# Output products between key pieces, weights requested first and a store awaited later in a decode step with windowed attention

## The reference

```python
# layer 0: latent attention | dilated window attention, one output projection
y = jnp.concatenate([o_mla, o_swa], axis=-1) @ w_out
# layer 1: gated short convolution
y = (b_gate * conv) @ w_out
# each layer
x = layer_norm(a*x + mixer(x)); x = layer_norm(a*x + mem_attend(x)); x = layer_norm(a*x + peer(x))

def dilated_group_attend(q_pos, q, kv_all, row0_pos, win, dil, bias):   # win, dil: (128,1) (512,4) (2048,16)
    s = jnp.einsum('bqhd,bqjhd->bhqj', q, kv[:, :, :, 0]) * SWA_SCALE + bias   # masked
    e = jnp.exp(s - m); den = e.sum(-1)
    o = jnp.einsum('bhqj,bqjhd->bqhd', e / den, kv[:, :, :, 1]); lse = m + log(den)

def mem_attend(x, kv, wq, wo):                       # 256 memory rows, 4 heads of 256
    s = jnp.einsum('bshd,bmhd->bhsm', x @ wq, kv[:, :, 0]) * MEM_SCALE
    return jnp.einsum('bhsm,bmhd->bshd', softmax(s), kv[:, :, 1]).reshape(B, S, D_MODEL) @ wo
```

## Time and profile before

| what | value |
|---|---|
| median of 3 runs | 2777.76 us (2771.65 to 2778.41) |
| the profiled execution, its own time | 2773.06 us |
| its span, first to last instruction | 2771.3 us |
| its mean granted TensorE clock | 0.972 |
| PE busy | 2592.0 us (94%) |
| DVE, ACT, POOL busy | 1428.2, 341.7, 621.0 us |
| moved by DMA | 885.35 MB, mean 319 GB/s |

### The profile page before, as it was taken

How to read it: one execution, slowest core, us unless ns; L and a number is a source line. 1 busy time by engine, 2 the same in 40 slices (tenths; PEclk the granted TensorE clock), 3 DMA queues, 4 the chain that set the end, 5 groups by cost and what they waited for, 6 DMA issues and landing times. The chain is left out here.

```text
span 2771.3 us, 40409 instructions
## 1 busy us (share of the span) xinstructions
PE 2592.0 (94%) x16081; PEld 2156.5 (78%) x16081; DVE 1428.2 (52%) x3384; ACT 341.7 (12%) x997; POOL 621.0 (22%) x619
## 2 busy tenths in 40 slices
PE   7889987799899999999999999988999999999997
PEld 5564464346399999999999866464999999999997
DVE  2430020122269979995555221222799799855553
ACT  3210120012021111110000010120211121100000
POOL 0005000000004324444333000000044244533330
PEclk9799998899999999999999999999999999999999
DMA  7789958996927999999999795769089899899995
GB/s 239 252 278 283 369 198 346 387 371 242 400 104 294 374 338 328 354 340 401 409 409 409 282 378 219 278 245 361 1 346 376 315 344 354 327 410 409 409 409 192
DMA packets 249128, 885.35 MB, mean 319 GB/s; under 512 B 27386, under 2 KB 34714, under 8 KB 238143
## 3 DMA queue, kind: packets, MB, share of 16 engines
q1 hardware_dynamic: 169374, 606.97, 58.7%
q0 software_dynamic: 79568, 275.81, 26.4%
HBM read 863.33 MB, written 109.08 MB: 351 GB/s over the span
## 5 line engine op out<-in xcount | busy, mean ns | idle before, releaser
L2891 PE MATMUL ps<-xT,front 128*128 128x192 f32 x4096 | 686.8, 327 | 3.5 <-DMA front<-in_peer_uT 2.9
L2891 PEld LDWEIGHTS ps<-xT,front 128*128 128x128 f32 x4096 | 663.1, 190 | 8.9 <-DMA front<-in_peer_uT 6.2
L2917 PE MATMUL ps<-p1e_S,p_qT 128*128 128x192 f32 x2048 | 336.9, 327 | 5.9 <-DMA p_qT<-in_peer_v 5.9
L2917 PE MATMUL ps<-p0e_S,p_qT 128*128 128x192 f32 x2048 | 337.0, 327 | 5.1 <-DMA p_qT<-in_peer_v 5.1
L2917 PEld LDWEIGHTS ps<-p1e_S,p_qT 128*128 128x128 f32 x2048 | 332.5, 190 | 10.0 <-DMA p_qT<-in_peer_v 10.0
L2917 PEld LDWEIGHTS ps<-p0e_S,p_qT 128*128 128x128 f32 x2048 | 332.4, 190 | 9.5 <-DMA p_qT<-in_peer_v 9.4
L2667 DVE CUSTOM_DVE_ANT_0 front<-front,x_tok 128x1024 f32<-128x1024 f32 x256 | 309.6, 1217 | 8.4 <-DMA front<-in_peer_u,p1e_expert 2.2
L2568 POOL DMA_INDIRECT front<-in_peer_u,p1e_expert x128 | 154.3, 1206 | 384.5 <-DVE p1e_dots L2667 200.7
L2568 POOL DMA_INDIRECT front<-in_peer_u,p0e_expert x128 | 154.0, 1203 | 385.0 <-DVE p0e_dots L2667 200.2
L2678 DVE SCALAR_TENSOR_TENSOR h_tok<-front,p1e_dots,h_tok 128x1024 f32<-128x1024 f32 x127 | 163.1, 1284 | 143.1 <-DMA front<-in_peer_v,p1e_expert 114.4
L2678 DVE SCALAR_TENSOR_TENSOR h_tok<-front,p0e_dots,h_tok 128x1024 f32<-128x1024 f32 x127 | 163.2, 1285 | 141.9 <-DMA front<-in_peer_v,p0e_expert 141.1
(11 more groups left out here) (474 smaller groups left out, 2855.1 us busy)
## 6 DMA issues: line engine op xcount, KB each, us to landing
front<-in_peer_uT SPq DMA_DIRECT2D x256, 512.0 KB
p_qT<-in_peer_v SPq DMA_DIRECT2D x256, 512.0 KB
out_swa_sample<-in_cache_swa_w SPq DMA_DIRECT2D x32, 2040.0 KB, 21.2
e_ring<-in_mla_pages SPq DMA_DIRECT2D x84, 272.0 KB, 4.6
e_ring<-in_swa_kT SPq DMA_DIRECT2D x16, 1024.0 KB, 7.8
e_arena<-in_swa_v SPq DMA_DIRECT2D x16, 1024.0 KB, 13.2
out_swa_sample<-in_cache_swa_w SPq DMA_DIRECT2D x8, 2016.0 KB, 31.1
e_ring<-in_attn_w_in SPq DMA_DIRECT2D x6, 2048.0 KB, 34.5
```

The source lines that it names most:

```text
L2891: mm = pe.matmul(k.ps[:, SB[i % len(SB)], 0:TD], ur[:, i % NU, c, :], k.xT[:, c, D0:T], start=(c == 0), stop=(c == KC - 1))
L2917: mm = pe.matmul(k.ps[:, c // 2, c % 2 * TD:(c % 2 + 1) * TD], vr[:, i % NV, c * P:(c + 1) * P], S[:, i, :], start=False, stop=(i == STEPS ...
```

## The change

Four edits in the layer 0 attention, and one in layer 1:

- The 16 products of a half are one sequence, cut over the twelve key pieces of the group: 11 of them behind pieces 2 to 12, one each (`products_beside`), and the last 5 behind the scores (`products_left`).
- The second half of the output weights is requested at the start of the sample stage, ahead of its first key request (`first`).
- The prompt stage no longer waits for its stores (`Stores` with due 0); the wait stands in the sample stage ahead of the first value request (`before_values`).
- The counts that the products wait for are given by hand: (64, 32).
- In layer 1 the ring "nx1" is allocated on the other side of the memory, and the room of the experts is opened before stage "nx1". Four key and two value transfers of the memory attention are requested there, behind load 2 (`load_early`); the prompt stage requests the other two values.

```diff
@@ joined_stage
                 ring.load(sp, n, job, i).then_inc(w_landed[n % NR], 16)
+                if beside_loads and n == beside_loads[0]:
+                    beside_loads[1](sp)
                 if n < len(copies):
                     k.copy_some(sp, copies[n])
@@ EarlyProjection
-    def product(self, pe, s, i):
-        pe.wait_ge(self.landed[s], self.due[s])
-        for c in range(KC):
-            mm = pe.matmul(self.k.ps[:, self.BANKS[i], :], self.aT[:, c, i * P:(i + 1) * P], self.pieces[s, c],
+    def products(self, pe, s, first, last):
+        for n in range(first, last):
+            i, c = divmod(n, KC)
+            if n == 0:
+                pe.wait_ge(self.landed[s], self.due[s])
+            mm = pe.matmul(self.k.ps[:, self.banks[i], :], self.aT[:, c, i * P:(i + 1) * P], self.pieces[s, c],
                            start=c == 0, stop=c == KC - 1)
-        mm.then_inc(self.tile_done, 1)
+            if c == KC - 1:
+                mm.then_inc(self.tile_done, 1)
+
+    def products_beside(self, pe, s, part, parts):
+        self.products(pe, s, part * self.BESIDE_SCORES // parts, (part + 1) * self.BESIDE_SCORES // parts)
+
+    def products_left(self, pe, s):
+        self.products(pe, s, self.BESIDE_SCORES, 2 * KC)
@@ attend_packed, SP
+            if a.get("first"):
+                a["first"](sp)
             for g in range(GROUPS):
                 for u in range(g * GB, (g + 1) * GB):
                     load_keys(u)
+                if g == 0 and a.get("before_values"):
+                    a["before_values"](sp)
                 for u in range(g * GB, (g + 1) * GB):
                     load_values(u)
-                if early and g == 0:
-                    early.load(sp, 1)
@@ attend_packed, PE
                     mm.then_inc(k_used, 1)
+                    if early:
+                        early.products_beside(pe, g, b * NPART + j, GB * NPART)
...
-                    if early and u == g * GB + 1:
-                        early.product(pe, g, 0)
                 if early:
-                    early.product(pe, g, 1)
+                    early.products_left(pe, g)
                     early.wait_taken(pe, g, 0)
@@ Stores
-        sp.wait_ge(self.sem, self.due)
+        if self.due:
+            sp.wait_ge(self.sem, self.due)
@@ even_mixer
-                    lambda sp: store_windows(k, kv, sp), k.window_stored, 16 * N_WINDOW_STORES,
+                    lambda sp: store_windows(k, kv, sp), k.window_stored, 0,
@@ swa_sample
-        "ahead": ahead, "early": early,
+        "ahead": ahead, "early": early, "first": lambda sp: early.load(sp, 1),
+        "before_values": lambda sp: sp.wait_ge(k.window_stored, 16 * N_WINDOW_STORES),
@@ MemoryCaches (new; load_keys and load_values as in memory_attention before)
+    def load_early(self, sp):
+        for u in range(self.keys_early):
+            self.load_keys(sp, u, u).then_inc(self.k.mem_keys_landed[u], 16)
+        for u in range(self.values_early):
+            self.load_values(sp, u, u).then_inc(self.k.mem_values_landed[u], 16)
@@ decode_step
-                ring = Ring(k, c2, "nx1", 3)
+                ring = Ring(k, c2, "nx1", 3, k.sb(rooms, "nx1_w", [P, 3, KC * 512], side="right"))
...
+                rooms.close()
+                room = ExpertRoom(k, rooms, 1)
+                caches = MemoryCaches(k, 1, room, keys_early=4, values_early=2)
                 joined_stage(k, "nx1", ring, conv_out, norm_of["mix"][1],
                              mid=[memory.values], last=[memory.queries], turn_at=1,
-                             copies=(0, 0, 2, 2, 2, 2))
+                             copies=(0, 0, 2, 2, 2, 2), beside_loads=(2, caches.load_early))
```

More of the change, by code:

```diff
@@ L374, in begin_next, with joined_stage @@
         self.ahead, self.first_slot = self.next_ahead, self.next_slot
-def joined_stage(k, name, ring, out_job, norm, mid=(), last=(), turn_at=0, memT=None, copies=(), zeros_behind=None, head=None, beside=None, next_job=None, rest=None):
+def joined_stage(k, name, ring, out_job, norm, mid=(), last=(), turn_at=0, memT=None, copies=(), zeros_behind=None, head=None, beside=None, next_job=None, rest=None, beside_loads=None):
     nc = k.nc
@@ L628, with __init__ @@
 class EarlyProjection:
-    BANKS = (4, 6)
-    def __init__(self, k, job, regions, first_due):
-        self.k, self.regions = k, regions
+    BESIDE_SCORES = 11
+    def __init__(self, k, job, banks, landed, due, regions):
+        self.k, self.regions, self.banks, self.landed, self.due = k, regions, banks, landed, due
         _, self.aT, self.w, self.chunk, _ = job
-        self.pieces, self.due = {}, [first_due, 0]
-        self.landed = [k.first_landed, None]
+        self.pieces = {}
         for s, region, c0, n in regions:
-            self.due[s] += 16
             for i in range(n):
@@ L2229, in load, with __init__, load_keys, load_values @@
         sp.dma_start(self.wq[n], src).then_inc(self.k.wq_landed[n], 16)
-def memory_attention(k, memory, ring, experts):
+class MemoryCaches:
+    def __init__(self, k, layer, room, keys_early=0, values_early=0):
+        self.k, self.layer, self.keys, self.values = k, layer, room.memory_keys, room.memory_values
+        self.keys_early, self.values_early = keys_early, values_early
+    def load_keys(self, sp, u, slot):
+        return sp.dma_start(self.keys[:, slot, :, :], self.k.io["mem_kT"][self.layer, u])
+    def load_values(self, sp, u, slot):
+        src = self.k.io["cache_mem_kv"][self.layer, u, :, 1].rearrange("(i p) h d -> p i (h d)", p=P)
+        return sp.dma_start(self.values[:, slot, :, :], src)
+    def load_early(self, sp):
[3 more added lines that the diff above has]
+            self.load_values(sp, u, u).then_inc(self.k.mem_values_landed[u], 16)
+    def load_ahead(self, sp):
+        for u in range(self.keys_early, 4):
+            self.load_keys(sp, u, u).then_inc(self.k.mem_keys_landed[u], 16)
+        for u in range(self.values_early, 4):
+            self.load_values(sp, u, u).then_inc(self.k.mem_values_landed[u], 16)
+def memory_attention(k, memory, ring, caches):
     nc, io, layer = k.nc, k.io, memory.layer
@@ L2236, in memory_attention @@
     with ExitStack() as ctx:
-        keys, cache = experts.memory_keys, experts.memory_values
+        keys, cache = caches.keys, caches.values
         queries = PackedQueries(k, qT)
[L2240 to L2251, removed]
         with ExitStack() as c1:
@@ L2270, in memory_attention @@
                                         mkv[:, :, :]).then_inc(k.mem_kv_stored, 16),
-                k.mem_kv_stored, 16 * (layer + 1), load_ahead, queries.gpsimd))
+                k.mem_kv_stored, 16 * (layer + 1), caches.load_ahead, queries.gpsimd))
         with ExitStack() as c1:
@@ L2291, in memory_attention @@
                 "k_due": lambda m: 16 * (2 * layer + m // 4 + 1), "v_due": lambda u, part: 16 * (2 * layer + u // 4 + 1),
-                "load_keys": lambda sp, u, part, slot: load_keys(sp, u, slot),
-                "load_values": lambda sp, u, part, slot: [load_values(sp, u, slot)],
+                "load_keys": lambda sp, u, part, slot: caches.load_keys(sp, u, slot),
+                "load_values": lambda sp, u, part, slot: [caches.load_values(sp, u, slot)],
                 "scores": scores, "values": lambda slot, kk, h: cache[:, slot, kk, h * MEM_D:(h + 1) * MEM_D],
@@ L2998, in decode_step @@
             ring = Ring(k, c1, "nm0", 2, room.ring)
-            memory_attention(k, memory, ring, room)
+            memory_attention(k, memory, ring, MemoryCaches(k, 0, room))
         peer(k, 0, room, front, NormBeforeExperts(k, 0, front, ring, memory.out, norm_of["mem"][0]), io["mem_wk"][1])
```

12 lines of the change are left out of this document (6 added, 6 removed).

## The result

| | before | changed |
|---|---|---|
| median of 5 runs | 2771.75 us (2771.01 to 2778.41) | 2752.60 us (2746.12 to 2760.87) |
| profiled execution, its own time | 2773.06 us | 2746.12 us |
| its span | 2771.3 us | 2744.3 us |
| granted TensorE clock in it | 0.972 | 0.980 |

The ratio is 0.9924 with a 95% interval of 0.9905 to 0.9943, which is 21 us (16 to 26) less. The forecast was 14.3 us less, 2761 us, with a range down to 2754; the sign and the mechanism hold, the size was too small. The two profiled executions differ by 27 us, more than the ratio, so part of that is not the change's.

A forecast was written before the change was run, and what follows sets the result against it. PE was busy 94% of the span, but in layer 0's sample attention the stream of cached keys and values set the pace. Gains of 11.0 (layer 0) and 3.3 (layer 1), 14.3 us off 2775.2, gave 2761 us, range 2754 to 2772.

The forecast's parts named there:

- The walk: Layer 0 sample attention: key and value landings followed in order; last values at 548.7 instead of 560.36, 11.7 us earlier.
- The store wait: End of layer 0's prompt stage: SP's 1.2 us wait for stores goes, so PE begins at 414.2 instead of 415.42.
- the 3.5 of the start: Start of layer 0's sample stage: weight requests go out at about 414.3, so DMA work starts 3.5 us sooner.
- layer 0's 11.0 us: Layer 0 sample attention: total gain of 11.0 us, from 11.7 less 0.7, bounds 5.5 and 12.7.
- 2.0 + 3.0 + 2.3 = 7.3 us: Layer 0 sample attention: queue holes at 436 to 446.6, 455.7 to 464 and 515.3 to 525, expected to go.
- upper bound of 12.7: Layer 0 sample attention: the most that its edits were expected to gain, 12.7 us.
- Layer 1's 3.3 us: Layer 1 memory attention: moved loads save 1.27 us of value wait and 2.0 before the output projection; bounds 0 and 3.6.
- base of 2775.2: Whole kernel: average of all four executions before, 2775.2 us, from which the forecast gain was subtracted.
- (b): Layer 0 sample attention: PE falls behind the keys, both value slots late, gain 8 us, 2767 us; chance 0.15.
- (c): Layer 0 sample attention: PE at its low clock throughout, 21 us slower, 2796 us; chance 0.04.
- limit of 38%: Layer 0 key pieces: PE keeps pace while under about 38% of the time is at the low clock.
- (d): Layer 0 sample attention: the queue's mean rate is the limit, holes not recovered, 4.5 us gain, 2770.7 us; chance 0.07.

The follow-up runs named there:

- 2 MB more: Changed kernel plus an unneeded 2 MB copy requested behind the second weights: ratio 0.9956 to the kernel before, stage 143.1 us.
- products in lumps: Changed kernel with layer 0's products again in two lumps of eight a group: median 2764.75 us, ratio 0.9961 to the kernel before.
- output weights early: Changed kernel with layer 1's memory output weights requested in the prompt half, behind the last two values: median 2754.01 us, ratio 0.9936 to before.
- changed kernel again: The changed kernel, unedited, measured a second time: ratio 0.9923 to the kernel before, stage 137.3 us.
- before, trace 3: The kernel before, unedited, traced a third time: single time 2766.66 us, stage 149.3 us.
- no product left: Changed kernel with all 16 products beside the twelve key pieces and none behind the scores: ratio 0.9934 to the kernel before, stage 137.5 us.

## Why the prediction was right in kind and too small

**Right.** The queue sets the end of the sample stage (2 MB more cost 5.7 us), PE's lumps and the start make its holes, and closing them is the gain. The walk holds against the profile after, when both are counted from the stages ahead, which were 3.3 us shorter in that execution: group 1's first key was forecast 9.0 us earlier and came 13.3 - 3.3 = 10.0 earlier, the last value wait was forecast 11.7 and came 15.9 - 3.3 = 12.5 earlier. The softmax is what is next behind the scores (2.90 us of waiting with nothing left beside it). The new place of the store wait and the moved memory loads cost nothing that any trace shows.

**The store wait**, forecast 1.2 us within the 3.5 of the start, is 1.1.

**The term that was mis-sized is layer 0's 11.0 us.** It measured 14.9 in the stage (mean of six old traces 152.2, less 137.3) and 1.1 ahead of it, 16.0 together. Three steps of it failed. First, I took 0.7 off for a PE that falls behind; none did. Second, and largest, the holes that the products make were read from one profile as 2.0 + 3.0 + 2.3 = 7.3 us, and its stage of 149.8 us was the second shortest of six. It had none at group 1's value slots, where the five others have 2.5 to 2.9 us; with the lumps put back the stage is 9.9 us longer. Third, I let everything behind the last value landing keep its distance to it. In the pair of profiles the last value matmuls began 4.86 us ahead of the first product of the 64 rows before and 3.71 after, and 32 of their records took 1.93 us (560.36) against 1.23 (544.50); over the six old and six changed traces the distance fell by 0.9 us on the mean. The upper bound of 12.7 assumed the old stage to be a fixed number. That pair alone gives 13.7 us: 12.3 in the stage and 1.3 ahead of it. The parts fit: 9.9 for the products, 4.9 for the weights first (152.2 less the 147.3 of products in lumps; 3.1 when the products are spread) and 1.1 for the stores are 15.9.

**Layer 1's 3.3 us** consisted of 1.27 and 2.0 up to the projection, which is 2.8 in the traces: the output weights landed later than I reckoned, 12.2 us after their request instead of 9.5, and output weights early shows that 1.1 us of wait were theirs. What I did not count is the projection itself. In the six traces with the old layer 1 it took 29.0 to 30.4 us, mean 29.4; in the eleven with the new one eight took 27.5 or 27.6 and three 29.0 or 29.1, mean 28.0. So 1.4 us more come on the mean, not every time, and no run shows why.

**The sum** is then 16.0 + 2.8 + 1.4 = 20.2 us, 0.9927 of 2774, against 0.9924 and 0.9923 measured. I also chose a base of 2775.2 where the five runs of before have a median of 2771.75; that is 3.5 of the 8.4 us by which the point was too high.

**The rivals.** (b) and (c), PE behind the keys, did not occur. From 420 on PE was busy for 74 to 95% of the windows with keys, with the queue full, and its granted clock was 1.00 in 420 to 450 and 500 to 510, and 0.91 in 480 to 500, which is 18% at 1.2 GHz. Only ahead of 420 was it busy throughout, at 0.82 (36% low), and there the queue's share rose to 1.04 and more all the same. Two of my sums were off: the limit of 38% is 35% by its own terms, 0.6/1.7, and the gain under (b) is 9.0 us by its terms and not 8. With products between the waits the clock was higher: 0.90 to 0.94 over the stage in the six changed traces, against 0.81 to 0.83 in the six old ones and 0.84 with only the products in lumps again. The Trainium skill, "TensorE: Matmul & The Clock Gate", section "Loop structure matters more than you think", warns of a long DMA wait between matmuls; here the pieces stood between waits of 0.6 to 2.5 us already (0.73 to 0.88), and the products filled them. (d), a limit on the mean rate, is refuted by 406 GB/s and a share of 1.01 from 420 to 548, and by the stage's mean rate, which rose from 367 to 400 GB/s. The 358 GB/s of the Trainium skill, "DMA: Bandwidth & Descriptors", section Bandwidth, did not bind here: 421 GB/s over 20 us. The same section gives 425 GB/s for 16 MB with one core alone, and 358 when both cores of a memory domain stream; this kernel runs on one core, and the trace agrees with that part. The prediction had cited only the other sentence.

## What to carry to other kernels

Where a stream of transfers sets the pace, look for the stretches in which its share is under 1 (the holes) and ask which slot it waits for; then cut the other work of the engine that frees the slots into pieces no longer than the wait for one transfer, and leave only as much in one run as a chain beside it takes. A transfer with nothing to wait for belongs where the queue would otherwise stand, even ahead of more urgent ones. And take a stage with holes from several traces: its length varied by 6 us here, and one profile tells neither its mean nor the bound of what closing the holes gives.

## What the runs showed of the hardware that I had not expected

The same stage repeats within 0.3 us (137.2 to 137.5 in six traces) when its queue hardly idles, and varies by 6.4 with holes.

In layer 1's output projection the first 3 us ran at a granted clock of 0.50 to 0.53 in nine traces and at 1.00 in eight, and it took 29.0 us or more in the nine and 27.6 in the eight. One pair of profiles suggests that the wait ahead of it decides. Windows of before (2.82 us of waiting) and of the changed kernel (1.92):

```profile
1898.00:1901.00 3.00, 2.96 (x4) 1.36 (x5) 0.00 (x0) 0.00 (x0) 0.00 (x0) 0.54 1.05 384
```

```profile
1876.70:1879.70 3.00, 2.94 (x7) 1.44 (x8) 0.00 (x0) 0.10 (x1) 0.00 (x0) 1.00 1.04 386
```

It does not. In the changed kernel again the wait is 2.82 us, and the projection starts at 1.00 and takes 27.7:

```profile
1880.73 27.73 PE L727 MATMUL ps<-p1e_S,front 128*128 128x512 f32 x64 [2.82 <-DMA p1e_S<-in_mem_wo]
```

```profile
1880.73:1883.73 3.00, 3.00 (x7) 1.43 (x8) 0.00 (x0) 0.00 (x0) 0.00 (x0) 1.00 1.04 382
```

And before, trace 3, with products in lumps and no product left wait 1.94, 1.98 and 1.79 us and start at 0.50 to 0.53. The old layer 1 started low in all six traces, the new one in three of eleven; why is open.

In layer 0, where that wait is of the same size in before and changed (2.67 and 2.82 us), the same projection took 27.6, 29.0 to 29.3 or 30.3 to 30.6 us from run to run, whatever the edit. So such a difference in one profile says nothing by itself.

What also stays open is why the stages ahead of the sample stage take 410.8 to 420.0 us in these traces; no edit touches them but the 1.1 us of the store wait.
